# Sample state updates as one pass over stacked high and low parts, exponent columns of four heads at once, constant loads by GpSimd, small matmuls spread, in a two-layer hybrid decoder step

## The reference

```python
x = x + 0.5 * swiglu(rmsnorm(x))                      # feed-forward 1
# mLSTM head, chunkwise; C is (dv, dk), carried from chunk to chunk
D = b_t - b_s + i_s                                   # masked to s <= t, b = cumsum(log f)
w = (q_t . k_s) * exp(D - m_t)
num = w @ v + exp(b + m - m_t) * (C q)
h = num / max(|den|, exp(-m_t))
wk = exp(b_last - b + i - m_new)
C_new = decay * C + (v * wk)^T k                      # 256 x 128, for every sample sequence
# GLA head
S_new = exp(b_last) * S + (k * exp(b_last - b))^T v
# RG-LRU branch, then x += W_out(gated sum), feed-forward 2
```

## Time and profile before

| what | us |
|---|---|
| median of 3 runs | 3417.94 |
| lowest, highest | 3417.92, 3419.95 |
| the profiled execution | 3412.85 |
| its span | 3411.1 |
| TensorE busy | 3305.5 |
| VectorE busy | 1889.6 |
| ScalarE busy | 1005.2 |

### The profile page before, as it was taken

How to read it: one execution, slowest core, us unless ns; L and a number is a source line. 1 busy time by engine, 2 the same in 40 slices (tenths; PEclk the granted TensorE clock), 3 DMA queues, 4 the chain that set the end, 5 groups by cost and what they waited for, 6 DMA issues and landing times.

```text
span 3411.1 us, 59165 instructions
## 1 busy us (share of the span) xinstructions
PE 3305.5 (97%) x25040; PEld 3229.7 (95%) x25040; DVE 1889.6 (55%) x2517; ACT 1005.2 (29%) x956; POOL 0.4 (0%) x9
## 2 busy tenths in 40 slices
PE   7999989999999989999999999999999999999997
PEld 7999989989999989999999999899899999899997
DVE  5434455556676875434454345555676678754344
ACT  4212222223232653212232123222333236432122
POOL 0000000000000000000000000000000000000000
PEclk9999999989999999999999999899899899999998
DMA  3222222232222212222222222222222222222222
GB/s 125 86 105 82 79 90 89 88 113 78 77 85 71 89 68 87 81 98 86 80 87 83 99 81 88 85 107 106 82 76 77 78 80 81 76 87 83 89 78 71
DMA packets 52057, 294.29 MB, mean 86 GB/s; under 512 B 9081, under 2 KB 12281, under 8 KB 23033
## 3 DMA queue, kind: packets, MB, share of 16 engines
q1 hardware_dynamic: 37296, 242.48, 20.8%
q10 hardware_dynamic: 14672, 50.60, 4.0%
HBM read 271.55 MB, written 21.50 MB: 86 GB/s over the span
## 4 chain that ended last, share of the span: by engine, by line
PE 79%; DVE 10%; ACT 6%; issue 3%; DMA 1%; ACTq 0%; DVEq 0%
PE stream_b L358 33%; PE stream_a L358 31%; PE stream_a L432 5%; PE mix L457 2%; ACT wh L703 2%; DVE wl L970 1%; PE stream_b L432 1%; PE mix L465 1%; PE mix L515 1%; DVE xc L1375 1%; PE mix L608 1%; PE mix L506 1%; PE mix L517 1%; DVE wS L1313 1%; ACT L884 1%
## 5 line engine op out<-in xcount | busy, mean ns | idle before, releaser
L703 ACT ACTIVATE wh<-stage 128x2048 fp32r<-128x2048 f32 (+2 forms) x246 | 435.9, 1773 | 838.7 <-PE stream_b L358 586.0
L970 DVE TENSOR_TENSOR wl<-stage,wh 128x2048 fp32r<-128x2048 f32 (+2 forms) x248 | 525.8, 2120 | 169.2 <-ACT wh L703 152.6
L358 PE MATMUL stream_a<-xh,wh 128*128 128x272 f32 x2560 | 547.1, 295 | 32.4 <-DVE wl L970 15.3
L358 PE MATMUL stream_b<-xh,wh 128*128 128x272 f32 x2560 | 538.0, 291 | 9.8 <-DVE lyg L961 7.4
L358 PE MATMUL stream_a<-xl,wh 128*128 128x272 f32 x2560 | 538.4, 292 | 0.0
L358 PE MATMUL stream_a<-xh,wl 128*128 128x272 f32 x2560 | 537.1, 292 | 0.0
L358 PE MATMUL stream_b<-xl,wh 128*128 128x272 f32 x2560 | 530.3, 289 | 0.0
L358 PE MATMUL stream_b<-xh,wl 128*128 128x272 f32 x2560 | 528.4, 288 | 0.0
L358 PEld LDWEIGHTS stream_a<-xh,wh 128*128 128x128 f32 x2560 | 412.6, 193 | 43.4 <-issue 25.4
L358 PEld LDWEIGHTS stream_b<-xh,wh 128*128 128x128 f32 x2560 | 403.9, 188 | 20.0 <-DVE lyg L961 8.6
L358 PEld LDWEIGHTS stream_a<-xh,wl 128*128 128x128 f32 x2560 | 411.5, 193 | 0.0
(11 more groups left out here) (303 smaller groups left out, 4746.9 us busy)
## 6 DMA issues: line engine op xcount, KB each, us to landing
stage<-in_w_up SPq DMA_DIRECT2D x88, 1024.0 KB, 4.8
stage<-in_w_mix SPq DMA_DIRECT2D x88, 1024.0 KB, 4.8
stage<-in_w_down SPq DMA_DIRECT2D x32, 768.0 KB, 4.2
stage<-in_w_down SPq DMA_DIRECT2D x32, 640.0 KB, 3.9
seven<-rows_scratch ACTq DMA_DIRECT2D x8, 1088.0 KB, 8.0
CS<-in_c ACTq DMA_DIRECT2D x8, 1024.0 KB, 4.7
out_o_sc<-CS ACTq DMA_DIRECT2D x8, 1024.0 KB
CS<-in_s ACTq DMA_DIRECT2D x8, 1024.0 KB, 4.8
```

The source lines that it names most:

```text
L358: mm = [pe.matmul(out(h), a(h), b(h), start=f, stop=z) for h in range(2)]
L703: act.activation(wh[:, slot, 0:width], stage[:, slot, 0:width], ACT.Copy).then_inc(hi_done, 1)
L970: tt_(wl[:, slot, 0:width], stage[:, slot, 0:width], wh[:, slot, 0:width].bitcast(F32), ALU.subtract).then_inc(split_done, 1)
```

## The change

Seven edits. (1) `four_parts` writes a 32-row tile four times onto 128 partitions: for the keys high, low, high, low, for the values high, high, low, low, both F32R. `Kws` becomes 128 rows, the mask of each sequence stands four times in `seqm`, and a sample update is one product of F32R tiles with 128 rows. In an mLSTM head the weight of a key is taken from the row sum of its exponentials (`w1`), and L529's product reads `Kf` and a padded mask `seq0`. (2) The first mLSTM head of a layer makes the exponent columns of all four heads with five products of four columns; later heads read theirs from `cols`. (3) Constants are loaded by GpSimd, behind the second half of x, which SP loads; there are 13 loads. (4) The first squares use two buffers, the first two weight blocks are split behind the second and fifth row block. (5) The decay rates are made behind the first half of feed-forward 1 of layer 0. (6) TensorE's small products stand inside tiles: the first sample output of an mLSTM head before the last two k tiles, updates 2 and 3 inside the last tile. (7) The small score tile has a buffer of its own with 128 rows, `wSs`, rows 32 up zero. `gstage` shares memory with the feed-forward's tiles.

```diff
-CONST_LOADS = 9
+CONST_LOADS = 13
@@ SP, GpSimd, ScalarE
+            sp.dma_start(x[:, KT // 2:KT, :], x_T[:, KT // 2:KT, :]).then_inc(x_loaded[1], 16)
+            pool.wait_ge(x_loaded[1], 16)
+            for dst, rows, copies in ((ident, P, 1), (ones, P, 1), (neg_p, P, 1), (neg_s, NS, 1),
+                                      (seqm, NS, P // NS), (reset, P, 1)):
+                    pool.dma_start(dst[g * rows:(g + 1) * rows, :],
+                                   consts[0:rows, col:col + width]).then_inc(const_loaded, 16)
...
+            act.dma_start(x[:, 0:KT // 2, :], x_T[:, 0:KT // 2, :]).then_inc(x_loaded[0], 16)
             act.wait_ge(init_done, 1)
...
-                act.activation(sq[:], x[:, m, :], ACT.Square).then_inc(sq_ready, 1)
-                if m in (0, 3):
+                if m > 1:
+                    act.wait_ge(acc_ready, m - 1)
+                act.activation(first_sq[m % 2][:], x[:, m, :], ACT.Square).then_inc(sq_ready, 1)
+                if m in (1, 4):
...
+                    if half == 0 and gates and L == 0:
+                        decay_rates()
...
-                    act.activation(Ex[:, sl], Ex[:, sl], ACT.Exp, bias=cols[:, c:c + 1])
+                    act.activation(Ex[:, sl], Ex[:, sl], ACT.Exp, bias=cols[:, ds(i + c * HEADS, 1)])
@@ TensorE
-                    mm = pe.matmul(Q[:, b_, e * DV:(e + 1) * DV], Kws[:, 2 * pair_ + e, :], val[0:NS, NC, 0:DV],
+                    mm = pe.matmul(Q[:, b_, e * DV:(e + 1) * DV], Kws[:, 2 * pair_ + e, :], V4[:],
...
-                pe.wait_ge(a_rows, B * 16 + 16)
-                for c in range(NC + 1):
-                    m = C if c < NC else NS
-                    mm = pe.matmul(Q[0:m, 2, 200 + c:201 + c], RB[0:1, 3, c * C:c * C + m], ones[0:1, 0:1],
-                                   start=True, stop=True)
+                if first:
+                    pe.wait_ge(rows_ready, L + 1)
+                    for c in range(NC + 1):
+                        row = merged[0:HEADS, 3, :]
+                        m = C if c < NC else NS
+                        mm = pe.matmul(Q[0:m, 2, 200 + c * HEADS:200 + (c + 1) * HEADS], row[:, c * C:c * C + m],
+                                       ident[0:HEADS, 0:HEADS], start=True, stop=True)
...
-                pair_block(n + 2, t + 4, 0, updates)
+                pair_block(n + 2, t + 4, 0, updates,
+                           ((), ((KT - 2, lambda: sample_out(0)),)))
...
-                pair_block(n + 3, t + 6, 1, mean)
+                def third():
+                    pe.wait_ge(head_samples, taken + 1)
+                    sample_updates(2, 2, a_us)
+
+                pair_block(n + 3, t + 6, 1, mean, ((), ((2, lambda: sample_updates(1, 3, a_us)), (6, third))))
                 pe.wait_ge(a_sqs, B + 1)
                 column_sum(hsq[:, 0], 0, a_var)
-                for e in (2, 3):
-                    pe.wait_ge(head_samples, taken + (e - 1))
-                    sample_updates(e, e, a_us)
+                pe.wait_ge(head_samples, taken + 2)
+                sample_updates(3, 3, a_us)
@@ VectorE
+                four_parts(V4, v_, (0, 1), (2, 3))
+
+            def four_parts(dst, src, high, low):
+
+                for g in high:
+                    ins = dve.tensor_copy(dst[g * NS:(g + 1) * NS], src)
+                link(ins)
+                for g in low:
+                    ins = tt_(dst[g * NS:(g + 1) * NS], src, dst[0:NS].bitcast(F32), ALU.subtract)
+                link(ins)
+
+            def masked_keys(src):
+
+                four_parts(K4, src, (0, 2), (1, 3))
+                return tt_(Kws[:], spread(K4[:].bitcast(F32).unsqueeze(1), 1, SEQS), spread(seqm[:].unsqueeze(2), 2, P),
+                           ALU.mult)
...
-                link(dve.tensor_copy(Kts[:], Q[0:NS, 2, NS:NS + P]))
-                tt_(Kws[:], spread(Kts[:].unsqueeze(1), 1, SEQS),
-                    spread(Ex[0:NS, T + TS - 1:N:TS].unsqueeze(2), 2, P), ALU.mult).then_inc(a_kw, 1)
+                link(dve.tensor_reduce(w1[0:NS], Ex[0:NS, T + TS - 1:N:TS], mybir.AxisListType.X, ALU.add))
+                link(ts_(Kf[0:NS], Q[0:NS, 2, NS:NS + P], w1[0:NS], None, ALU.mult))
+                masked_keys(Kf[0:NS]).then_inc(a_kw, 1)
...
-                tt_(Kws[:], spread(Q[0:NS, 1, P:2 * P].unsqueeze(1), 1, SEQS),
-                    spread(seqm[:].unsqueeze(2), 2, P), ALU.mult).then_inc(b_took, 1)
+                masked_keys(Q[0:NS, 1, P:2 * P]).then_inc(b_took, 1)
...
+                link(dve.memset(val[:, NC, 0:DV], 0.0))
+                link(dve.memset(Kf[:], 0.0))
```

159 lines of the change are left out of this document (90 added, 69 removed).

## The result

| | before | after |
|---|---|---|
| median | 3418.64 us (4 runs, 3417.92 to 3419.95) | 3363.8 us (4 runs, 3361.78 to 3370.96) |
| ratio | | 0.9843, 95% interval 0.9826 to 0.986 |
| profiled execution, span | 3412.85, 3411.1 us | 3364.34, 3362.5 us |

The kernel is 54.8 us faster by the medians and 48.5 us by the profiled executions. The prediction said 24.2 us and 3394 us, with a range of 3374 to 3413 us.

A forecast was written before the change was run, and what follows sets the result against it. TensorE, busy 3305.5 of 3411.1 us, was taken as the bound. Terms of -7.0 - 26.5 + 17.3 - 16 + 8 = -24.2 us, applied to the median 3417.94, gave 3394 us, range 3374 to 3413.

The forecast's parts named there:

- 1. The opening: Opening: fewer ScalarE loads, two square buffers and later decay rates start the third tile at 32.8 us; -7.0 us.
- that rival: Opening: constants moved to GpSimd arrive after the square products need them, so the opening's gain is lost; 3405 us, chance 0.07.
- 2 and 3. Products and parts: mLSTM and GLA heads: cheaper sample products save 26.5 us; splitting values and keys on VectorE costs 17.3 us.
- the rest costs nothing visible: Remaining edits, such as the states' copy and GpSimd's thirteen constant loads, have no visible cost.
- Step 2: Sample products in mLSTM and GLA heads: each falls from 0.48 to 0.119 us, partly hidden by waits; -26.5 us.
- 4. The clock: mLSTM heads: spreading small products cuts half clock, -16 us; longer idle time ahead of the update products costs +8 us.
- The rival in which the longer wait makes TensorE slow: mLSTM heads: 3.1 us idle brings half clock through the tile into the small products; 3442 us, chance 0.05.
- The sign to look for: GLA heads: longer by 0 to 1 us, listed among the signs that the forecast is right.

The follow-up runs named there:

- a_early: Changed kernel with an mLSTM head's update products released once Kf is made, ahead of the key parts and Kws; 3339.7 us.
- b_pad: Kernel before the change with only the score x value products of both kinds of heads padded to 128 rows; 3386.9 us.
- a_rows32: Changed kernel with the padded score x value and keys x mask products back on 32 rows; 3383.3 us.
- a_high32: Changed kernel with sample updates as one-pass products of the high parts alone, on 32 rows instead of 128; 3383.6 us.
- a_nospread: Changed kernel with TensorE's small products of an mLSTM head back outside the tiles; 3382.5 us.
- g_old: Changed kernel with the GLA heads' small products as before the change, mLSTM heads and opening as changed; 3378.9 us.
- a_root: a_early with ScalarE's root ahead of its next weight-block copy in GLA heads, VectorE's split later, TensorE's column sum ahead of two sample updates; 3319.4 us.

## Why the prediction was wrong, step by step

**1. The opening** (-7.0, measured -6.7, and -8.1 in a_early, which has the same opening): right in sum, not in its parts. I had the third tile at 32.8 us; it came at 35.85 (34.50 in a_early), since the first weight block landed only at 11.5 us and the last square sum ended at 26.65 us, not 25.1. What saved the sum is a gain that I had not priced: TensorE no longer idles ahead of the third tile, which so runs at full clock, 2.7 us less. The decay rates, which I had as 3.7 us of it, were worth 2.3. The constants were in time, so that rival fell: GpSimd issues one load in 0.5 to 0.7 us, the last issue ends at 16.2 us, and each load landed 2.2 to 4.7 us later, against square products at 28.42. The Trainium skill, "SBUF — State Buffer", section "Who interferes with whom", gives VectorE's two-input operations no mode that would hold such loads up, and the trace agrees.

**2 and 3. Products and parts** (-9.6 in the mLSTM stage, measured -18.4 at full clock). From the update products to the next head the mLSTM heads take 26.6 us less at full clock, forecast 19.7; from the scores to the update products 8.6 us more, forecast 10.1. The pass count was right (two updates take 0.24 us, as forecast), and so were VectorE's parts: 282 and 417 ns for the operations on values, 1.24 us later update products in six heads in place of 0.7, 0.8 to 1.1 us a GLA head in the ring in place of 0.9.

```profile
L1171 DVE TENSOR_TENSOR Kws<-K,seqm 128x1024 fp32r<-128x1024 f32 x16 | 19.6, 1226 | 0.6
...
L1165 DVE TENSOR_TENSOR V<-val,V 32x256 fp32r<-32x256 f32 x32 | 13.4, 417 | 0.8
...
L1162 DVE CAST V<-val 32x256 fp32r<-32x256 f32 x32 | 9.0, 282 | 0.8
```

The step that failed is 5, "the rest costs nothing visible": I listed the 128-row score tile as an edit and gave it no price. By b_pad and a_rows32 it is worth 6 to 8 us in the mLSTM stage at full clock, about the 8.8 us that are missing. Step 2 failed in the same way on a smaller point: it priced an update by itself (0.48 to 0.12 us) and not what a 32-row product costs its neighbours. The 12.4 us of a_high32 can't be added to the 8 us, because the 0.12 us of the forecast is already that of a 128-row product and part of the 12.4 comes from the spreading.

**4. The clock.** The net of -8 in the mLSTM stage became -1.7. By place, behind the update products the loss falls from 31.2 to 11.3 us, 19.9 less; I had -16 for the spreading, a_nospread gives 13.5 for it, and b_pad shows that the padding, which I had at nothing, takes off 6.7 too. In the update products the loss rises from 1.7 to 14.1 us; I had +8, from 1 us in each head at waits of up to 2.5 us, and the waits became 4.0 us on average. The last 5.9 us more are lost ahead of them, in part in idle time, where they cost nothing. The rival in which the longer wait makes TensorE slow was right in that the wait brings half clock, and wrong in how far it lasts: in seven of eight heads it covers most of the update products (1.4 to 2.4 us lost), and the tile behind them loses 0.2 us at most, so it never reaches the small products.

The larger failure is that step 4 counts half clock in the mLSTM heads alone and puts the GLA stage at nothing, without a reason; the runs showed 18.6 us less lost there, most of it behind the outputs and through the heads' own products (g_old). The rows for the GLA stage were as near: 0.92 and 0.93 over 693 us are 50 us lost, more than the 41.4 us of the mLSTM stage (for which I had 28), beside the same small products that I had argued with. How much of the 18.6 us comes from the heads and how much from the pattern of spells that the kernel ahead hands over stays open within several us.

**The sign to look for.** I wrote that GLA heads would get longer by 0 to 1 us. The time from their first score product to the outputs did (22.6 to 23.7 us), and the stretch behind it became 3 us shorter.

## What to carry to other kernels

Price the row height of small products. One on 32 rows between products on 128 cost 0.1 to 0.4 us for the change each way here, and in three of the four stages of a_rows32 and b_pad more time was lost to half clock with it; filling it up with zeros cost nothing. The one product that stood behind a wait gained nothing from it. An edit that puts more small groups between wide products changes what each of them costs, so their prices don't simply add. Where the mean granted clock is below 1, work out the time lost in every stage before you say which edit touches it, and add to an idle time ahead of TensorE what the products right behind it lose at half clock: here 20 us less waiting took another 12.5 us off those products. And look at what each queue does between the last input and the result that the slowest engine waits for: two releases put in front (a_early and a_root) gave 44 us, nearly as much as the whole change.

## What the runs showed that I had not expected

- Lost time comes in spells. One stretch of the same instructions takes 20.6, 22.3 or 23.9 us, and in both layers mostly the same one.
- What a stage loses also hangs on what stands before it. The changed GLA heads lost 30.6 to 45.9 us in eight kernels that differ only elsewhere. A single edit of 10 us in such a kernel can't be judged by its median alone; here the sum by stages was needed. What picks the pattern stays open: two shifts of the start, by 1 and 2.9 us, moved the loss by 5.6 and -1.3 us, and neither gave the 45 us of a_nospread and a_early.
- Padding 40 products of the kernel before was worth 30.5 us by the medians but 17.4 us by its profiled execution, so a single profile of such a kernel can be some 10 us off.
